# Twenty-four of the 64 units in the first half of a product get split weights

## The reference, cut to what matters

```python
def chunk(xc):
    qh = (xc @ wq).reshape(PEER_CHUNK, PEER_HEADS, 2, PEER_HALF)
    s1 = jnp.einsum('thd,kd->thk', qh[:, :, 0], sub_keys[0])
    s2 = jnp.einsum('thd,kd->thk', qh[:, :, 1], sub_keys[1])
    v1, i1 = lax.top_k(s1, PEER_TOPK)
    v2, i2 = lax.top_k(s2, PEER_TOPK)
    cand = v1[..., :, None] + v2[..., None, :]      # 16 x 16 sums for each head
    best, pos = lax.top_k(cand, PEER_TOPK)          # the selection
    expert = jnp.take_along_axis(cidx, pos, axis=-1)
    gate = jax.nn.softmax(best, axis=-1)
    u_sel, v_sel = u[expert], v[expert]             # rows of 2048
    act = gelu(jnp.einsum('td,thkd->thk', xc, u_sel))
    return jnp.einsum('thk,thkd->td', gate * act, v_sel)
```

## Time and profile before

| what | value |
|---|---|
| median of 3 runs | 3026.83 us (3018.61 to 3031.2) |
| the profiled execution's own time | 3026.03 us |
| its span, first to last instruction | 3024.1 us |
| PE busy | 2846.4 us, 94% |
| DVE busy | 1903.4 us, 63% |
| ACT busy | 1408.8 us, 47% |
| granted TensorE clock, mean | 0.975 |
| U1, first and last product | 1707.0 and 2083.4 us |
| V1, first product | 2092.0 us |
| U2, first product | 2390.6 us |
| V2, first product | 2689.1 us |
| first product after V2 | 2998.1 us |

### The profile page before, as it was taken

One profiled execution on the slowest core, in us unless ns is written; L12 is line 12 of the kernel. 1 busy time (PEld: TensorE's weight loads), 2 busy tenths in 40 slices (PEclk: granted clock), 3 DMA queues, 4 the chain that ended last, 5 costly groups with the idle time before them and its releaser, 6 DMA issues.

```text
span 3024.1 us, 46453 instructions
## 1 busy us (share of the span) xinstructions
PE 2846.4 (94%) x19394; PEld 2681.0 (89%) x19394; DVE 1903.4 (63%) x2801; ACT 1408.8 (47%) x2399; POOL 362.9 (12%) x338
## 2 busy tenths in 40 slices
PE   6999998798999999999989999998999999999996
PEld 6999998687888999999988999998887899988775
DVE  5546647642333544656456855776888888878886
ACT  5346544355555433443335204433555555545554
POOL 0000010011112000002200002222122111112210
PEclk9999999899999999999999999999999999999998
DMA  4444435422232554444434458998999988889984
GB/s 185 169 157 145 171 103 178 150 98 73 78 100 94 204 181 169 167 168 158 157 127 156 152 203 312 371 362 325 366 361 363 357 326 317 324 333 345 357 338 142
DMA packets 112048, 668.47 MB, mean 221 GB/s; under 512 B 28336, under 2 KB 28552, under 8 KB 33920
## 3 DMA queue, kind: packets, MB, share of 16 engines
q1 hardware_dynamic: 86976, 496.93, 45.4%
q0 software_dynamic: 23712, 164.11, 14.8%
q10 hardware_dynamic: 1152, 4.47, 0.4%
HBM read 651.54 MB, written 13.30 MB: 220 GB/s over the span
## 4 chain that ended last, share of the span: by engine, by line
PE 66%; DVE 13%; DMA 10%; ACT 7%; issue 2%; SPq 0%; POOL 0%; DVEq 0%; ACTq 0%
PE PS L1001 66%; DMA raw<-in_pv 8%; DVE WL L1626 5%; DVE m L1617 3%; ACT WH L2304 3%; ACT m L2289 2%; DMA m<-in_pv,keep 1%; DVE m L2129 1%; ACT L2289 1%; DVE m L1817 1%; DMA raw<-in_w_kv 1%; DVE m L1814 0%; ACT m L2290 0%; PE PS L1004 0%; DVE m_896r L2222 0%
## 5 line engine op out<-in xcount | busy, mean ns | idle before, releaser
L1626 DVE TENSOR_TENSOR WL<-raw,WH 128x1024 fp32r<-128x1024 f32 x804 | 985.5, 1233 | 672.8 <-ACT WH L2304 671.9
L2304 ACT CAST WH<-raw 128x1024 fp32r<-128x1024 f32 x804 | 837.3, 1046 | 571.2 <-PE PS L1001 371.6
L1001 PE MATMUL PS<-m_4096r,WH 128*128 128x256 f32 x5184 | 997.9, 293 | 31.1 <-DVE m_4096r L1617 11.5
L1001 PEld LDWEIGHTS PS<-m_4096r,WH 128*128 128x128 f32 x5184 | 827.1, 196 | 54.7 <-issue 13.2
L1001 PE MATMUL PS<-m_4096r,WL 128*128 128x256 f32 x2592 | 743.5, 287 | 0.0
L1001 PE MATMUL PS<-m_8192r,WH 128*128 128x256 f32 (+1 forms) x2560 | 561.1, 313 | 16.7 <-issue 11.1
L1001 PE MATMUL PS<-WH,m_896r 128*128 128x512 f32 x1536 | 524.1, 394 | 24.6 <-DVE m_896r L2222 24.5
L1001 PEld LDWEIGHTS PS<-m_4096r,WL 128*128 128x128 f32 x2592 | 507.1, 196 | 0.0
L1001 PEld LDWEIGHTS PS<-m_8192r,WH 128*128 128x128 f32 x2560 | 398.6, 194 | 19.6 <-issue 11.7
L1001 PE MATMUL PS<-m_8192r,WL 128*128 128x192 f32 (+1 forms) x1792 | 405.1, 273 | 0.0
L1001 PE MATMUL PS<-WL,m_896r 128*128 128x512 f32 x1024 | 401.5, 392 | 0.0
(11 more groups left out here) (228 smaller groups left out, 1869.7 us busy)
## 6 DMA issues: line engine op xcount, KB each, us to landing
raw<-in_pu SPq DMA_DIRECT2D x128, 1024.0 KB, 6.9
raw<-in_pv SPq DMA_DIRECT2D x128, 1024.0 KB, 8.7
raw<-in_w_qkv SPq DMA_DIRECT2D x48, 1024.0 KB, 4.8
raw<-in_w_o SPq DMA_DIRECT2D x48, 1024.0 KB, 4.8
raw<-in_w SPq DMA_DIRECT2D x40, 1024.0 KB, 4.8
raw<-in_w_z SPq DMA_DIRECT2D x32, 1024.0 KB, 4.9
raw<-in_w_kv SPq DMA_DIRECT2D x16, 1024.0 KB, 4.8
raw<-in_w_q SPq DMA_DIRECT2D x16, 1024.0 KB, 4.8
```

Source lines behind the costliest of these rows:

```text
L1001: return e.matmul(o, l, x, start=start, stop=stop)
L1626: tt(WL[:, k, :], raw[:, n % NRAW, h * 1024:h * 1024 + 1024], WH[:, k, :].bitcast(F), ALU.subtract).then_inc(S["lo"], 1)
L2304: e.copy(WH[:, k, :], raw[:, n % NRAW, h * 1024:h * 1024 + 1024]).then_inc(S["hi"], 1)
```

## The change

Before, all units of U1 are plain. Now `merged(j)` names 24 of them: j = 1, 3, ... 31 (16 units) and j = 35, 39, ... 63 (8 units). They are no longer plain: their weights are split by ACT and DVE as everywhere else, PE multiplies them with 384 and 192 columns, ACT copies the second 192 columns of the result out of PSUM (`u_copy`), DVE adds them to the first (`u_sum`, into `UF`, a place in `vec`), and the gelu reads the sum. The counts of the semaphores `lo`, `hi` and `u_sum` follow. The gathered steps of U1 go from 0.13 to 0.09 for each part, those of U2 from 0.05 to 0.08. By the sequence of steps U1, V1, U2 and V2 have 41, 33, 25 and 29 gathers before and 28, 33, 41 and 26 after.

```diff
-SPARSE_RATE = (0.13, 0.26, 0.05, 0.29)
+SPARSE_RATE = (0.09, 0.26, 0.08, 0.29)
...
+def merged(j):
+
+    return j % 2 == 1 if j < 32 else j % 4 == 3
+
+
 def plain(n):
 
-    return PEER <= n < PEER + 64
+    return PEER <= n < PEER + 64 and not merged(n - PEER)
+
+
+SPLIT = list(accumulate(0 if plain(q // 2) else 1 for q in range(2 * NUNIT)))
 
 
 def split(q):
 
-    return q + 1 - min(max(q + 1 - 2 * PEER, 0), 128)
+    return SPLIT[q]
+
+
+def sums(half, j):
+
+    return sum(merged(i) for i in range(64 if half else j + 1)) + (j + 1 if half else 0)
...
+        UF = vec[:, 0:ND]
...
             def u_sum(half, j):
-                if half == 0:
+                if half == 0 and not merged(j):
                     return
-                v.wait_ge(*at("u_copy", j + 1))
-                if j >= 2:
+                v.wait_ge(*at("u_copy", sums(half, j)))
+                if half and j >= 2:
                     v.wait_ge(*at("gelu_gated", count["gated"]))
-                tt(uz_of(j), PS[:, U_BANK[j % 3], 0:ND], ux_of(j), ALU.add).then_inc(S["u_sum"], 1)
+                o, x = (uz_of(j), ux_of(j)) if half else (UF, UF)
+                tt(o, PS[:, U_BANK[j % 3], 0:ND], x, ALU.add).then_inc(S["u_sum"], 1)
...
             def u_sum(half, j):
-                if half == 0:
+                if half == 0 and not merged(j):
                     return
-                a.wait_ge(*at("used", done(PEER + 128 + j)))
-                if j >= 2:
-                    a.wait_ge(*at("u_sum", j - 1))
+                a.wait_ge(*at("used", done(PEER + 128 * half + j)))
+                if half and j >= 2:
+                    a.wait_ge(*at("u_sum", sums(1, j - 2)))
+                elif half == 0:
+                    for name in ("gelu", "gelu_gated"):
+                        if count[name]:
+                            a.wait_ge(*at(name, count[name]))
...
-                e.copy(ux_of(j), PS[:, U_BANK[j % 3], ND:2 * ND]).then_inc(S["u_copy"], 1)
+                e.copy(ux_of(j) if half else UF, PS[:, U_BANK[j % 3], ND:2 * ND]).then_inc(S["u_copy"], 1)
 
             def u_out(half, j, tq):
                 x = PS[:, U_BANK[j % 3], 0:ND]
-                if half:
-                    a.wait_ge(*at("u_sum", j + 1))
-                    x = uz_of(j)
+                if half or merged(j):
+                    a.wait_ge(*at("u_sum", sums(half, j)))
+                    x = uz_of(j) if half else UF
                 else:
                     a.wait_ge(*at("used", done(PEER + j)))
```

More of the change, by code:

```diff
@@ L2 @@
 from contextlib import ExitStack
+from itertools import accumulate
 import numpy as np
@@ L1126, in feed @@
                 else:
-                    p.wait_ge(*at("u_sum", j - 2))
+                    p.wait_ge(*at("u_sum", sums(1, j - 3)))
                 return None, None, U_BANK[j % 3], True, True
@@ L1565, in c_begin @@
                 if half:
-                    p.wait_ge(*at("u_sum", 64))
+                    p.wait_ge(*at("u_sum", sums(1, 63)))
                     p.wait_ge(*at("acc_v", 4))
@@ L2595, in sp_gate @@
                 act(DOT, DOT, ACT.Gelu).then_inc(S["sp_gelu"], 1)
-            count = {"gated": 0}
+            count = {"gelu_gated": 0, "gelu": 0}
             def g_hots(q, j):
@@ L2644, in u_out @@
                 if tq:
-                    if count["gated"] >= 2:
-                        a.wait_ge(*at("gated", count["gated"] - 1))
-                    count["gated"] += 1
-                    act(gt_of(count["gated"] - 1)[:, 0:tq], x[:, 0:tq], ACT.Gelu).then_inc(S["gelu_gated"], 1)
+                    if count["gelu_gated"] >= 2:
+                        a.wait_ge(*at("gated", count["gelu_gated"] - 1))
+                    count["gelu_gated"] += 1
+                    act(gt_of(count["gelu_gated"] - 1)[:, 0:tq], x[:, 0:tq], ACT.Gelu).then_inc(S["gelu_gated"], 1)
                 if tq < ND:
+                    count["gelu"] += 1
                     a.wait_ge(*at("st_h", 16))
@@ L2655, in c_split @@
                 a.wait_ge(*at("g_apply", NQ))
-                a.wait_ge(*at("gated", count["gated"]))
+                a.wait_ge(*at("gated", count["gelu_gated"]))
                 if j >= 2 or half:
```

## The result

The changed kernel takes 3053.42 us (median of 4 runs, 3050.99 to 3056.65). The kernel before, run in turn with it on the same chip, takes 3022.72 us. The ratio is 1.0091 with a 95% interval of 1.0066 to 1.0116, which is 27 us more (20 to 35). The forecast was 3057.0.

The account below looks back on a forecast made before the run. PE was taken to bound U1 and U2, fully busy, with DVE and DMA near. The terms -15 + 21 + 4 + 12 + 10 - 1 = +31 on 3026.0 us gave 3057 us, range 3020 to 3082.

Parts of the forecast that it names:

- products: In U1, 24 merged units each take PE 0.63 us less: -15 us.
- waits, selection: PE waits for DVE in units 0 to 24 of U1: +21 us (bounds 8 and 24).
- clock: PE's clock falls after idle time, about 1.5 us lost each, four waits over 3 us: +4 us (0 to 9).
- waits, gates: PE waits for DVE's gate steps in 12 merged units, 25 to 63, mean 1.05 us: +12 us (3 to 22).
- U2: U2 gets 16 more gathers, with DMA and DVE nearly full: +10 us (3 to 20).
- V2 and end: V2 has 3 gathers fewer, so they end some five units earlier: -1 us.
- hand-over to V1: One copy and one sum more where U1 passes to V1: 0.7 us.
- tally (a): Unit 12: DVE's steps end 6.3 us into the unit, PE's transpose stands at 2.6: wait 3.7 us.
- the tally of ACT: Before merged unit n, ACT's first cast ends 1.3 us into unit n-1; after copy and gelu, the second at 3.2.
- Rival 1: No waits in U1, as DVE and ACT reach the casts early enough: 3013 us; chance 0.13.
- Rival 3: DVE at 97% bounds U2 and can't make up for late loads, U2 +33 us: 3080 us; chance 0.10.
- Rival 2: Break-even: half the selection waits, a quarter of the gates', no clock loss, little in U2: +3, 3029 us; chance 0.15.

Follow-up runs that it names:

- below 25 alone: The changed kernel with merged units only at j = 1, 3, ... 23 and the old gather rates; 1.0045 against the kernel before, +14 us.
- the 18 units: The changed kernel with casts and remainders half a unit later and units 5, 7, 13, 17, 19, 25 plain again; 0.9998 against the kernel before.
- the split alone: The changed kernel's merged units with the old gather rates (0.13 in U1, 0.05 in U2); 1.0080 against the kernel before, +24 us.

## Why the prediction was right, point by point

The measured time, 3053.4, lies in the range, slower by more than a measurement can fail to tell, and 3.6 us below the forecast. That the two are so near is luck for a good part. Terms were off by up to 8 us on both sides; together those of the change come to +18.9 where +31 was forecast, and the rest of the 27.4 of the spans lies in stages that the change does not touch and in 2.1 us of U1 that no term explains. The direction, the place of most waits and their cause were right. The terms against what the profiled executions show:

| term | predicted | measured | by |
|---|---|---|---|
| products | -15 | -14.8 (-13.3 with 1.5 us of waits in it) | casts left out |
| waits, selection | +21 | +20.2 | timeline of PE |
| clock | +4 | +8.4 | windows of 1 us, while PE worked |
| waits, gates | +12 | +3.8 | timeline of PE |
| U2 | +10 | +6.8 | stages |
| V2 and end | -1 | -3.1 | stages |
| hand-over to V1 | 0.7, not in the sum | -2.4 | idle at V1's first product |
| sum | +31 | +18.9 | |

The 8.5 us from there to the 27.4 of the spans are the differences before U1 and in V1 (3.7 and 2.7), which the change doesn't touch, and 2.1 that the terms of U1 leave open.

**Selection.** The mechanism was right, and the timeline shows most of the places that were named. That the sum came so near (20.8 and 20.2) is luck in part, as errors of 1.0 to 2.0 us cancelled. One by one: unit 5 predicted 0.5, measured 0.54; unit 7 3.2 and 2.7, measured 2.83 and 2.03; unit 17 1.4, measured 0.91; unit 19 4.2, measured 3.84. The others were off:
- Unit 20: 1.1 predicted for its transpose, none measured. The waits at transposes that I had not seen stand in units 11 (0.96) and 23 (1.19); both are for DVE's reduction (`s_add`), which comes behind the remainders of these units.
- Unit 12: 3.7 predicted, 1.92 measured. The wait of 0.96 in unit 11 makes unit 12 begin later, and DVE is nearer to PE by that: the first cast of unit 13 ends 0.2 us behind the start of unit 12 and not 1.3. This is read from the rows, not tried. The tally (a) started from an undisturbed PE.
- Unit 24: 4.0 predicted, 6.00 measured. Here is ACT in the changed kernel, in the half unit that decides:

```profile
1847.63 1.05 ACT L2321 CAST WH<-raw 128x1024 fp32r<-128x1024 f32 x1 [5.37 <-DMA raw<-in_pu]
1848.70 1.28 ACT L2306 ACT_TABLE_LOAD   x1
1850.50 0.31 ACT L2306 ACTIVATE m<-m 128x128 f32<-128x128 f32 x1 [0.52 <-DVE m L2118]
...
1851.04 1.28 ACT L2306 ACT_TABLE_LOAD   x1
1852.33 0.33 ACT L2306 ACTIVATE m<-PS 128x192 f32<-128x192 f32 x1
1852.56 1.04 ACT L2321 CAST WH<-raw 128x1024 fp32r<-128x1024 f32 x1
```

The first cast waits 5.37 us for its load. Between the two casts of unit 25 stand the exp of the softmax and a gelu, each with a table load of 1.28 us. The exp waits for DVE's step `s_exp`, which comes behind the first remainder, and so starts 1.8 us after the first cast (the first table load passes meanwhile); the second table load adds its 1.28. The second cast ends at 1853.6, which is 4.7 us into unit 24, where the tally had 3.2. DVE is queued behind it:

```profile
1848.71 1.23 DVE L1642 TENSOR_TENSOR WL<-raw,WH 128x1024 fp32r<-128x1024 f32 x1 [3.52 <-ACT WH L2321]
...
1853.63 1.23 DVE L1642 TENSOR_TENSOR WL<-raw,WH 128x1024 fp32r<-128x1024 f32 x1 [2.22 <-ACT WH L2321]
...
1855.32 0.29 DVE L2127 TENSOR_TENSOR m<-m 128x128 f32<-128x128 f32 x1
```

The last row ends at 1855.6, and PE's transpose begins at 1855.67. Less than a microsecond of DVE's work for the gates stands behind a remainder that nobody needs for another unit. What failed here is the tally of ACT: I had counted on it only casts, copy and gelu, and not the exp with its wait for DVE and the table load behind it. DVE's steps ended 6.8 us into unit 24 and not 5.3. The other half microsecond is a misread place: PE stood at the transpose 0.8 us into the unit, after an eighth of it, and not after a quarter (1.3). The kernel with units from 25 on alone, at 6.52 us, is the same place again. That the casts of unit 25 decide is shown by the kernels in which unit 25 is plain, with 0.9 us in both (below 25 alone, and the 18 units). The shares of the exp and of the table load in it were read, not tried.

**Clock.** The step that failed is the size: I priced four restarts at some 1.5 us and took a part off. There were four falls, but not behind the four waits that I had named: they stand behind the two waits of unit 7 (2.83 and 2.03 us), behind 3.84 and 6.00, and behind the 1.93 of unit 53, and PE's work lost 1.7, 2.8, 2.2 and 1.7 us to them, 8.4 in all. With 1.6 us of waits (18 units) no window of U1 is under 1.00. What part of the lost clock was given back by shorter waits cannot be read from these runs, but the balance of U1 leaves nothing for it: -14.8 + 24.0 + 8.4 = 17.6, and the stretch without the idle time of the hand-over grew by 19.7 (376.7 to 396.4).

**Gates.** +12 came out as +3.8. Two steps failed. The landing of loads is one: I took the 6.9 us of U2, and the changed kernel has 6.2 in this stage. For unit 35, worked out at 2.1 us, that leaves 1.4, and the timeline has 1.25. The other is the multiplication: I took the mean of unit 35 and unit 51 for all twelve merged units and had each microsecond of landing move twelve places. There are three waits in all, and only that of unit 35 stands in a merged unit. From 6.2 to 8.5 us of landing (the old rates) the waits grow from 3.8 to 13.0, which is 4 us for a microsecond and not 12; at 6.9 that gives some 6.6, an estimate from these two. The direction was right, and the prediction had named the landing as what would make the sum wrong most easily.

**U2.** The direction was right, but the place was not. By V1's percentage the cadence should have gone over 4.7; it went from 4.56 to 4.61. Of the 6.8 us of the column, 4.8 stand at the start of V2, where the idle time grew from 3.04 to 7.83 us, and 2.0 ahead of it. The step that failed was to take 373 GB/s as what full engines move and V1's 357 as what is had: U2 ran at 372 GB/s for 240 us with PE full. The page of the Trainium skill cited there, "DMA: Bandwidth & Descriptors", puts the limit of HBM at about 358; the trace does not agree, with 372 over 240 us (one core ran here). And the two stages belong together: in the three kernels with the old rates U2 and V2 to the end take 632.4 us in the mean (630.3 to 633.4), in the nine with the new rates 636.2 (631.7 to 640.2). By these means the move costs U2 and V2 some 4 us; the ranges overlap, and the kernel with the rates alone (+3, -3 to +9) does not settle it.

**Rivals.** Rival 1, no waits, is what comes about with the casts left out (-9), not with them in. Rival 3, DVE as the bound of U2, fell: DVE is at 92% there and the cadence has hardly moved, though DVE behind a late load is what V2's first product waits for. Rival 2 had half the waits and no loss of clock, at +3. The kernel with the later casts has about its waits in the selection (12.6 us) and fewer in the gates, but still loses 6.8 us to the clock, and takes +14.

**What stays open.** The hand-over to V1: the idle time there was 5.9 us after, 8.3 before and 11.8 with the split alone, and I did not try why. The loss of clock could not be tried apart from the waits that bring it.

## What to carry to other kernels

An engine with room in its sum can still be late: list what stands between the wait of a new operation and the next thing the bound engine needs from that queue, with table loads and with what each step waits for itself, and give each new wait its place. Work on a buffer that frees late belongs as late in the order as its consumer allows (half a unit later brought back half of the loss, with not one operation less, though it made one new wait where DVE was full), or on units whose buffer frees early. And a relief that is had by moving work to another stage is to be paid there: the moved gathers saved 9 us of waits in U1 and seem to have cost about 4 in U2 and V2.

## What the runs showed of the hardware

- Short gaps of PE can bring the clock down, and their length alone doesn't tell which will. Windows of the changed kernel just behind a gap, the last columns are clock, DMA share and GB/s: behind a single gap of 2.83 us, behind that and another of 2.03 us within five microseconds, behind one of 1.92 us, behind one of 3.84 us, behind a single one of 1.93 us:

```profile
1749.00:1751.00 2.00, 1.97 (x14) 2.00 (x15) 1.86 (x5) 0.00 (x0) 0.00 (x0) 1.00 0.61 258
...
1755.00:1757.00 2.00, 2.00 (x9) 2.00 (x9) 2.00 (x5) 0.00 (x0) 0.00 (x0) 0.50 0.86 336
...
1785.00:1787.00 2.00, 2.00 (x15) 2.00 (x14) 1.76 (x6) 0.00 (x0) 0.00 (x0) 1.00 0.01 5
...
1820.00:1822.00 2.00, 1.56 (x6) 1.59 (x7) 2.00 (x5) 0.36 (x1) 0.00 (x0) 0.50 0.36 152
...
2042.00:2044.00 2.00, 2.00 (x8) 2.00 (x7) 1.90 (x4) 1.80 (x5) 0.90 (x2) 0.50 0.66 123
```

The kernel with the split only, behind the gap of 2.45 us at 1978.43:

```profile
1979.00:1981.00 2.00, 2.00 (x18) 2.00 (x17) 2.00 (x5) 0.00 (x0) 0.15 (x1) 1.00 0.86 344
```

0.50 is the lower of the two levels, 1.2 GHz. It was there after 2.83 and 2.03 us of idle time close together, after 3.84, and after 1.93 alone. It was not there after 2.83, 1.92 or 2.45 alone. With the later casts it was there behind the 1.92 of unit 12 as well (1778 to 1780). The clock stayed low for three to six microseconds each time. What else decides was not found out.

- The DMA engines carried 372 GB/s over 240 us at a share of 0.96 while PE stayed fully busy and loads still landed in 7.8 us in the median.
- A subtraction of 128x1024 on POOL takes 2.50 us (mean of 26), where DVE takes 1.22, and DVE's operations beside it take up to ten times as long (0.23 to 2.29 us). An engine that was busy for 12% of the span was no free one.
